# Causal mask by a selection of GpSimd on the exponentials, and the decay input in four column groups of the array

## What is computed

```python
h = rms_norm(x, g_pre)
proj = h @ w_in       # q_a, k_a, v_a, z_a, q_b, k_b, v_b, z_b, lr (16 columns), gate_a, gate_b
# branch A: differential attention, 4 heads, two maps per head, causal
s = where(dist >= 0, q @ k * scale - slope * dist, -inf)
p = softmax(s);  pd = p[map 0] - lam * p[map 1];  oa = pd @ v
ya = (rms_norm(oa, g_sub_a) * (1 - lam_init) * silu(z_a)) @ w_up_a
# branch B: gated linear attention with a state, in chunks
glog = log_sigmoid(lr @ w_alpha + b_alpha) / 16
ob = chunked_linear_attention(q_b, k_b, v_b, glog)
yb = (rms_norm(ob, g_sub_b) * silu(z_b)) @ w_up_b
y = sigmoid(gate_a) * ya + sigmoid(gate_b) * yb
out = x + rms_norm(y @ w_out, g_post)
```

## Time and profile before

| what | value |
|---|---|
| median of 3 runs | 1799.26 us (1796.78 to 1802.73) |
| the profiled execution's own time | 1797.91 us |
| its span on the slowest core (core 6) | 1796.3 us; all cores 1782.6 to 1796.3 us |
| granted TensorE clock of that core, mean | 0.936 of 2.4 GHz |
| PE busy | 1492.4 us (83%) |
| DVE, ACT busy | 892.6 us (50%), 865.6 us (48%) |
| POOL busy | 154.0 us (9%) |

### The profile page before, as it was taken

One profiled execution on the slowest core, in us unless ns is written; L12 is line 12 of the kernel. 1 busy time (PEld: TensorE's weight loads), 2 busy tenths in 40 slices (PEclk: granted clock), 3 DMA queues, 4 the chain that ended last, 5 costly groups with the idle time before them and its releaser, 6 DMA issues.

```text
span 1796.3 us, 27798 instructions; the slowest of 8 cores (1782.6 to 1796.3 us)
## 1 busy us (share of the span) xinstructions
PE 1492.4 (83%) x10323; PEld 751.0 (42%) x10512; DVE 892.6 (50%) x2340; ACT 865.6 (48%) x1714; POOL 154.0 (9%) x231
## 2 busy tenths in 40 slices
PE   2775587779978898789987899888998889998877
PEld 1333233334434443444444444444454445444433
DVE  3467556564556345563446434364334561334464
ACT  3251345314452445335563455744667547667512
POOL 1011111010101001010000000000001010000011
PEclk9896799999999998999999999999999999999979
DMA  9674387413351325313252122521224311214113
GB/s 266 192 222 139 95 274 213 134 58 112 126 185 49 102 85 179 103 58 96 96 177 80 60 95 95 165 83 60 74 86 170 95 48 59 71 51 150 48 58 106
DMA packets 76368, 207.26 MB, mean 115 GB/s; under 512 B 9024, under 2 KB 27728, under 8 KB 76240
## 3 DMA queue, kind: packets, MB, share of 16 engines
q1 hardware_dynamic: 65376, 172.03, 31.6%
q0 software_dynamic: 8928, 32.51, 4.6%
q10 hardware_dynamic: 1936, 0.94, 0.2%
HBM read 172.94 MB, written 32.51 MB: 114 GB/s over the span
## 4 chain that ended last, share of the span: by engine, by line
PE 62%; DVE 23%; ACT 6%; DMA 4%; issue 3%; POOL 2%; ACTq 0%; SPq 0%; POOLq 0%; DVEq 0%
PE ps_f L268 37%; PE ps_q L268 11%; PE ps_oa L268 11%; DMA sb_KT<-w_in 3%; DVE sb_gtA L1000 2%; DVE sb_tmpo L975 2%; DVE sb_gtB L743 2%; DVE sb_junk L729 1%; DVE sb_state L719 1%; DVE sb_yT L676 1%; ACT sb_PT L950 1%; DVE sb_junk L990 1%; DVE sb_scr L646 1%; DVE sb_ATs L699 1%; ACT sb_wring L376 1%
## 5 line engine op out<-in xcount | busy, mean ns | idle before, releaser
L950 ACT ACTIVATE sb_PT<-ps_q 128x512 bf16<-128x512 f32 (+3 forms) x1152 | 580.8, 560 | 622.1 <-PE ps_q L268 621.1
L268 PE MATMUL ps_f<-sb_hT,sb_wring 128*128 128x512 bf16 x1542 | 413.6, 395 | 44.5 <-DVE sb_junk L990 7.4
L268 PE MATMUL ps_oa<-sb_V,sb_PT 128*128 128x129 bf16 x4224 | 347.9, 225 | 3.9 <-DVE sb_tmpo L975 2.9
L268 PEld LDWEIGHTS ps_oa<-sb_V,sb_PT 128*128 128x128 bf16 x4224 | 283.6, 100 | 131.5 <-issue 47.9
L268 PE MATMUL ps_f<-sb_wring,sb_hT 128*128 128x512 bf16 x938 | 248.2, 390 | 21.9 <-DVE sb_vb L658 3.7
L268 PE MATMUL ps_q<-sb_QT,sb_KT 64*128 64x512 bf16 (+3 forms) x1152 | 229.6, 380 | 11.3 <-ACT sb_PT L950 11.2
L268 PEld LDWEIGHTS ps_f<-sb_hT,sb_wring 128*128 128x128 bf16 x1624 | 143.1, 100 | 193.7 <-issue 91.5
L268 PEld LDWEIGHTS ps_q<-sb_QT,sb_KT 64*128 64x128 bf16 x1152 | 58.0, 93 | 200.9 <-issue 182.4
L268 PEld LDWEIGHTS ps_f<-sb_wring,sb_hT 128*128 128x128 bf16 x992 | 86.4, 100 | 108.6 <-issue 45.4
L794 DVE SCALAR_TENSOR_TENSOR sb_scr<-sb_scr,ps_f 128x512 f32<-128x512 f32 x59 | 40.4, 685 | 170.4 <-PE ps_f L268 170.4
L268 PE MATMUL ps_f<-sb_wring,sb_yT 128*128 128x512 bf16 x459 | 118.7, 385 | 2.9 <-issue 0.8
(11 more groups left out here) (129 smaller groups left out, 1510.9 us busy)
## 6 DMA issues: line engine op xcount, KB each, us to landing
sb_wring<-wsc SPq DMA_DIRECT2D x204, 512.0 KB, 3.8
sb_xb<-x SPq DMA_DIRECT2D x60, 512.0 KB, 4.2
sb_KT<-w_in SPq DMA_DIRECT2D x88, 256.0 KB, 8.0
out<-sb_xb POOLq DMA_DIRECT2D x32, 512.0 KB, 3.2
wsc<-sb_wring POOLq DMA_DIRECT2D x30, 512.0 KB, 7.7
sb_KT<-w_out SPq DMA_DIRECT2D x16, 256.0 KB, 8.2
sb_KT<-w_up_a SPq DMA_DIRECT2D x8, 256.0 KB, 8.3
sb_KT<-w_up_b SPq DMA_DIRECT2D x8, 256.0 KB, 8.6
```

The lines of the kernel that those rows point to most:

```text
L268: P.op("pe", lambda e: e.matmul(out=out_, lhsT=lhsT, rhs=rhs, start=start, stop=stop, **kw), reads=reads, writes=writes)
L950: act(lambda e, m=m: e.activation(out=PT[pp][:, m, c0:512], in_=BANK[banks[m]][:, c0:512], func=AF.Exp, bias=cbias, scale=1.0), [banks[m]] ...
```

## The change

Three things are edited. (1) The two mask matmuls of a diagonal step and their constant are gone; in their place one `affine_select` of GpSimd, behind the two exponentials, sets to zero the entries above the diagonal in `PT`, both maps in one instruction of 128 x 2 x 128. It reads and writes both keys of `PT`, so all products with V of that block wait for it. (2) The 8 matmuls of the decay input had 16 output columns each and one accumulator on partitions 0 to 15. They now have 32 (16 of zeros) and go to four column groups of the array, partitions 32 g to 32 g + 31 of the same bank, two accumulating in each group. DVE copies 128 partitions instead of 16, and the matmul with `walpha` sums the four groups, since its 16 rows stand four times in a matrix of 128 rows with zeros between. (3) The cost given for the chain is 0.08 a matmul instead of 0.26, which moves side units among steps. At the start there are three more small DMAs for `w_alpha` and one less for the mask, two more fills of POOL and three more copies of DVE.

```diff
-        wlr = SB("wlr", [128, 8, 16], BF16)
-        walpha = SB("walpha", [16, 256], BF16)
+        wlr = SB("wlr", [128, 8, 32], BF16)
+        walpha = SB("walpha", [128, 256], BF16)
...
-        lrT = gtB[0:16, :, :].rearrange("p a b -> p (a b)")
+        lrT = gtB[:].rearrange("p a b -> p (a b)")
...
-                               (walpha_st, w_alpha, "ztmp"), (lamv_st, lamv_d, "oaf"), (tri[:], tri_d, "tri"),
-                               (negm[:], negm_d, "negm"), (eft[:], ef_d, "eft"), (rmask[:], rmask_d, "rmask"),
+                               (ztmp[0:16, 0:256], w_alpha, "ztmp"), (ztmp[32:48, 0:256], w_alpha, "ztmp"),
+                               (ztmp[64:80, 0:256], w_alpha, "ztmp"), (ztmp[96:112, 0:256], w_alpha, "ztmp"), (lamv_st, lamv_d, "oaf"), (tri[:], tri_d, "tri"),
+                               (eft[:], ef_d, "eft"), (rmask[:], rmask_d, "rmask"),
...
+        pool(lambda e: e.memset(wlr[:], 0.0), [], ["wlr"])
+        pool(lambda e: e.memset(walpha[:], 0.0), [], ["walpha"])
...
-            dve(lambda e: e.tensor_copy(out=walpha[:], in_=walpha_st), ["ztmp"], ["walpha"])
+            for g in range(4):
+                dve(lambda e, g=g: e.tensor_copy(out=walpha[32 * g:32 * g + 16, :], in_=ztmp[32 * g:32 * g + 16, 0:256]),
+                    ["ztmp"], ["walpha"])
...
             def lr_one(b, k, st_, sp_):
-                mm(BANK[b][0:16, :], wlr[:, k, :], hT[t % 2][:, k, :], st_, sp_, ["wlr"] + hkeys(t), [b])
+                g, half = k % 4, k // 4
+                mm(BANK[b][32 * g:32 * g + 32, :], wlr[:, 2 * g + half, :], hT[t % 2][:, 2 * g + half, :], half == 0, half == 1,
+                   ["wlr"] + hkeys(t), [b])
 
             def lr_ev(b):
-                dve(lambda e: e.tensor_copy(out=lrT, in_=BANK[b][0:16, :]), [b], ["gtB"])
-
-            u_lr = chain(8, lr_one, lr_ev)
+                dve(lambda e: e.tensor_copy(out=lrT, in_=BANK[b][:, :]), [b], ["gtB"])
+
+            u_lr = chain(8, lr_one, lr_ev, 0.08)
...
-            if r >= 0:
-                for m in range(2):
-                    mm(BANK[banks[m]][:, c0:c0 + 128], ident[:, :], negm[:, :], False, True, ["ident", "negm"], [banks[m]],
-                       skip_group_check=True)
             pp = kb % 2
             cbias = SLOPES[h] * (128.0 * r - 129.0)
             for m in range(2):
                 act(lambda e, m=m: e.activation(out=PT[pp][:, m, c0:512], in_=BANK[banks[m]][:, c0:512], func=AF.Exp, bias=cbias, scale=1.0),
                     [banks[m]], [f"PT{pp}_{m}"])
+            if r >= 0:
+                pool(lambda e: e.affine_select(out=PT[pp][:, :, c0:c0 + 128], in_=PT[pp][:, :, c0:c0 + 128], pattern=[[0, 2], [1, 128]],
+                                               compare_op=ALU.is_ge, fill=fillreg[0], base=0, channel_multiplier=-1),
+                     [f"PT{pp}_0", f"PT{pp}_1"], [f"PT{pp}_0", f"PT{pp}_1"])
```

More of the change, by code:

```diff
@@ L25 @@
 C_QA, C_KA, C_VA, C_ZA, C_QB, C_KB, C_VB, C_ZB, C_LR, C_GA, C_GB = 0, 512, 1024, 1536, 2048, 2304, 2560, 3072, 3584, 3600, 4624
-NEG = -30000.0
 NPIECE = 7
@@ L163, in _build @@
     tri_d = din("tri", [128, 128], BF16)
-    negm_d = din("negmask", [128, 128], BF16)
     ef_d = din("eftab", [128, 4])
@@ L211, in _build @@
         tri = SB("tri", [128, 128], BF16)
-        negm = SB("negm", [128, 128], BF16)
         eft = SB("eft", [128, 4], F32)
@@ L238, in _build @@
         wlr_st = oaf[:, 3, :].rearrange("p (kc c) -> p kc c", kc=8)
-        walpha_st = ztmp[0:16, 0:256]
         psQ = [PSM(f"q{i}", [128, 512], F32) for i in range(3)]
@@ L328, in _build, with first_pool @@
         consts("act", "cstB", [(wlr_st, w_in[:, C_LR:C_LR + 16].rearrange("(kc p) c -> p kc c", p=128), "oafw"),
-                               (walpha_st, w_alpha, "ztmp"), (lamv_st, lamv_d, "oaf"), (tri[:], tri_d, "tri"),
-                               (negm[:], negm_d, "negm"), (eft[:], ef_d, "eft"), (rmask[:], rmask_d, "rmask"),
+                               (ztmp[0:16, 0:256], w_alpha, "ztmp"), (ztmp[32:48, 0:256], w_alpha, "ztmp"),
+                               (ztmp[64:80, 0:256], w_alpha, "ztmp"), (ztmp[96:112, 0:256], w_alpha, "ztmp"), (lamv_st, lamv_d, "oaf"), (tri[:], tri_d, "tri"),
+                               (eft[:], ef_d, "eft"), (rmask[:], rmask_d, "rmask"),
                                (gpost[:], gpost_d, "gpost")])
-        pool(lambda e: e.memset(lams[:, 5:6], -0.5), [], ["nhalf"])
+        fillreg = []
+        def first_pool(e):
+            fillreg.append(e.to_reg(0.0))
+            return e.memset(lams[:, 5:6], -0.5)
+        pool(first_pool, [], ["nhalf"])
+        pool(lambda e: e.memset(wlr[:], 0.0), [], ["wlr"])
+        pool(lambda e: e.memset(walpha[:], 0.0), [], ["walpha"])
         pool(lambda e: e.memset(state[:], 0.0), [], ["state"])
@@ L348, in setup_small @@
             dve(lambda e: e.tensor_scalar(out=nbal[:], in0=smalls[:, 10:12], scalar1=-1.0, scalar2=None, op0=ALU.mult), ["smalls"], ["nbal"])
-            dve(lambda e: e.tensor_copy(out=walpha[:], in_=walpha_st), ["ztmp"], ["walpha"])
+            for g in range(4):
+                dve(lambda e, g=g: e.tensor_copy(out=walpha[32 * g:32 * g + 16, :], in_=ztmp[32 * g:32 * g + 16, 0:256]),
+                    ["ztmp"], ["walpha"])
             for kc in range(8):
-                dve(lambda e, kc=kc: e.tensor_scalar(out=wlr[:, kc, :], in0=wlr_st[:, kc, :], scalar1=smalls[:, kc:kc + 1],
+                dve(lambda e, kc=kc: e.tensor_scalar(out=wlr[:, kc, 0:16], in0=wlr_st[:, kc, :], scalar1=smalls[:, kc:kc + 1],
                                                      scalar2=None, op0=ALU.mult), ["oafw", "smalls"], ["wlr", "oaf"])
@@ L1102, in _host_consts @@
     tri = (q >= k).astype(np.float32)
-    negm = np.where(k > q, NEG, 0.0).astype(np.float32)
     rmask = np.ones((128, 512), np.float32)
@@ L1108, in _host_consts @@
         "tri": tri.astype(bf),
-        "negmask": negm.astype(bf),
         "eftab": np.stack([np.exp(SLOPES[h] * (np.arange(128) - 127.0)) for h in range(4)], axis=1).astype(np.float32),
```

## The result

The change made the kernel slower: 1828.25 us (median of 4, the lowest 1824.98) against 1800.99 us before, ratio 1.0145 with a 95% interval of [1.0107, 1.0183]. I had forecast 1788 us. Before the experiments, the new profile already answers most of the signs that the prediction named.

What follows compares the result with a forecast made beforehand. PE, busy 83% of 1796.3 us, was taken to bound the kernel, early stages partly by waits. Masks -13, decay input -9.5, selection +9, start +1.5 and DVE +0.5 gave -11.5 us: 1788 us, range 1778 to 1807.

Steps and rivals of the forecast that it cites:

- the signs that the prediction named: Changed profile: selection's mean duration, waits for it of 5 to 12 us, decay matmuls starting together, DVE's busy time.
- The moved side units: Side units placed in other steps by the planner's changed cost: either sign, 3 us.
- Small terms: Extra DMA issues +0.9 and DVE copies +0.6 at the start, together +1.5 us; DVE beside POOL's copy +0.5.
- The mask matmuls: PE time of 128 pairs of mask matmuls removed, 80% of it returning: -13 us.
- The selection, its duration: One selection on POOL takes 0.7 us, range 0.4 to 2.0.
- my table of stalls: PE's stalls by selection duration, from 6.7 us at 0.5 to 39.2 us at 2.0.
- The selection, who waits: Products with V on PE wait for POOL's selection, over half of it in four places: +9 us.
- The decay input: Its matmuls in four column groups stream together, 90% of 10.8 us returning: -9.5 us.
- a slow selection: Rival: a selection on POOL of 1.6 to 2.0 us, stalls 26.9 to 39.2, total 1806 to 1818; chance 0.18.
- DVE isn't shut out: Rival: DVE instructions with two SBUF inputs wait until POOL's selection ends, up to 11 us, total 1799; chance 0.05.
- the groups do overlap: Rival: the decay input's column groups don't overlap, gaining 0 instead of 9.5 us, total 1797.5; chance 0.12.
- PE's time not given back: Rival: PE's waits for DVE stay; 5 us remain of the masks, 7 of the decay input, total 1798.5; chance 0.09.

Runs made afterwards that it cites:

- e1_keys: The changed kernel with a separate key for each of the four w_alpha DMAs, cost still 0.08; ratio 1.0053 to the kernel before.
- e5_all_oldcost: The changed kernel with four separate DMA keys and the chain's cost back at 0.26; ratio 0.9966 to the kernel before.
- e2_cost: The kernel before with only the planner's cost of the decay chain set to 0.08; ratio 1.0111.
- e9_first: The kernel before with the selection, only diagonal products waiting for it and coming last, and the selection moved ahead of roots and casts on POOL's queue; ratio 0.9982.
- e3_select: The kernel before with the selection on GpSimd in place of the mask matmuls and nothing else; ratio 1.0004.
- e4_groups: The kernel before with the decay input in four column groups and four DMA keys, old cost, masks by matmul; ratio 0.9969.
- e6_nomask: The kernel before without the mask matmuls and nothing in their place, so the causal mask is left out; ratio 0.9932.

## Why the prediction was wrong, point by point

- **Failed: "The moved side units: either sign, 3 us."** Measured +15.7 (e1_keys against e5_all_oldcost) and +20 (e2_cost alone). I had seen that the cost moves side units and even named them as a place where I could be wrong, but gave them a number without reading what stands behind the moved units. In the runs PE is idle 14 to 17 us longer in stages 2 to 7, and busy 2 to 8 us longer; why a cost of 0.12 or less does this and 0.17 doesn't stays open.
- **Failed: "Small terms", the start.** I priced the DMA issues at 0.45 us each. The issues cost about that (2.01 us for four); the wait of each for the landing of the one before cost 12.7 us more at ACT's first instruction (20.22 against 7.55) and 16.6 in the run. None of my rivals had a wait there. These two steps and the smaller gain of the three edits by themselves (-6.1 instead of -11.5) are the whole distance: 15.7 + 16.6 + 5.4 = 37.7 us between the forecast and +26.1.
- **The mask matmuls, -13:** right, -12.2.
- **The selection, its duration:** 0.42 instead of 0.7, inside the range. The Trainium skill ("GPSIMD Engine Reference", 3.1) had led to an estimate of 0.38 to 0.56 us; the trace agrees. What I said such a time would take off the sum, about 1 us, was too little: my table of stalls has 6.7 us at 0.5 against 9.1 at 0.7.
- **The selection, who waits, +9:** measured some +13 (1.0004 against 0.9932, with an uncertainty of 5 us), +9.8 in stages 2 to 7. The direct wait for POOL was right in its places, four of five named, and in its mechanism, since e9_first's other order on POOL took most of it away. That its total is 9.0 us, as my +9, is partly luck: at 0.42 us my table gives under 6.7, and with the side units in their old places e3_select has 7.9. The term that the sum lacked is the clock, about 5 us. With the masks it makes 0 where I had -4, so the selection as such isn't worth its edit.
- **The decay input, -9.5:** the groups overlap fully (0.33 us for four). 16 halves x 0.63 = 10.1 us of PE time; the gain of e4_groups is 5.6 [1.8, 9.2], with the start's +1.4 in it 7.0, and 7.4 in stages 2 to 7. Right within what can be told, though the 7 us of the rival fit as well. The Trainium skill ("TensorE: Matmul & The Clock Gate", Part 3, Measured speedup vs the span model) has 2.38 times for three column tiles; here four tiles took 0.33 us where four matmuls one after the other took 0.96, 2.9 times, the switches of mode included.
- **The rivals:** none held. The one that I gave most, a slow selection, was furthest off. DVE isn't shut out to the extent of that rival, and the groups do overlap. One rival, PE's time not given back, had -5 for the masks and -7 for the decay input; e6_nomask has -12.2 [-16.6, -8.1] for the masks. Without the two faults the kernel came to 0.9966, 1795 us, between my forecast and no change.

## What to carry to other kernels

Where a framework orders by key, look at what key each added DMA or copy writes: several transfers into parts of one buffer under one key run one landing after the other, and where they stand ahead of an engine's first work the whole kernel waits (here 15.47 us for four issues, 2.01 with a key each). A number that a planner uses is an edit of its own: measure it alone, and keep the old value until it is measured, even where the new one is nearer to the true duration. Read the granted clock of both kernels before PE time that was freed is counted as won: with the selection PE ran 11.4 us longer at the lower clock than without masks, some 5 us of time that no list of waits shows.

## What the runs showed of the hardware

- A selection of 128x256 in bf16 takes POOL 0.42 us, less than its copy of 128x256 from f32 to bf16 (0.49).
- Four matmuls of 512 columns on four column groups hold the array for 0.33 us, as long as the two of scores on row groups (0.32).
- With the same three waits of PE (1.3 to 1.4, 1.4 and 2.5 us) and the same 5.13 us of busy time in the 10 us that end with the last, the granted clock fell to 0.50 in one kernel and stayed at 1.00 in another, on all eight cores of each.
- DVE's instruction for `gtB`, 128x128 with two inputs from SBUF, takes 0.48 us beside a selection of POOL and 0.35 without one.
- Three DMAs of 16 KB on ACT's queue, each waiting for the one before, started 3.4, 6.7 and 5.0 us after it; with a key each, all four were issued in 2.01 us.
